# One core, two transformer-like blocks: the first norm's statistics taken token by token from x, and the first weights in two units

## The reference

```python
h = jnp.concatenate([meta, x], axis=1)            # 528 x 1024
y = xf * lax.rsqrt(jnp.mean(xf * xf, axis=-1, keepdims=True) + EPS)   # rmsnorm(h, norm1_g)
z = y * g
proj = z @ w_in[l]                                # 1024 x 5632
q, fl, iv, og, pin, ga, gb = jnp.split(proj, SPLITS, axis=-1)
```

## Time and profile before

| | us |
|---|---|
| median of three runs | 1639.83 |
| the profiled execution | 1643.81 |
| its span | 1642.0 |
| TensorE busy (matmuls) | 1563.1 (95%) |
| TensorE weight loads | 1369.9 (83%) |
| VectorE busy | 817.2 (50%) |
| ScalarE busy | 704.7 (43%) |

### The profile page before, as it was taken

The page is one execution under the profiler, slowest core; times in us unless marked ns, Lnnn a source line. Parts: engine busy times, 40 slices in busy tenths (PEclk is TensorE's granted clock), DMA queues, the critical chain, the costliest instruction groups (busy, mean ns, idle before and its releaser), DMA issues.

```text
span 1642.0 us, 24062 instructions
## 1 busy us (share of the span) xinstructions
PE 1563.1 (95%) x10314; PEld 1369.9 (83%) x10314; DVE 817.2 (50%) x1198; ACT 704.7 (43%) x1051; POOL 3.5 (0%) x14
## 2 busy tenths in 40 slices
PE   6999899999999999999999899899998999899988
PEld 5989899999998889997888667688897777678878
DVE  6376776645635445543345567532223555533243
ACT  4464666754324233232323655432222666633232
POOL 0000000000000000000000000000000000000000
PEclk9999899999998999999999999999999999799999
DMA  4421112114322323322324100122321111122222
GB/s 140 141 68 59 52 59 72 52 40 143 103 82 73 103 79 102 100 80 89 99 85 108 26 27 1 52 83 97 103 78 55 53 48 52 52 64 87 93 77 77
DMA packets 130957, 125.46 MB, mean 76 GB/s; under 512 B 20201, under 2 KB 128516, under 8 KB 130468
## 3 DMA queue, kind: packets, MB, share of 16 engines
q1 hardware_dynamic: 130388, 120.36, 23.4%
q0 software_dynamic: 464, 3.56, 0.6%
HBM read 119.66 MB, written 4.26 MB: 75 GB/s over the span
## 4 chain that ended last, share of the span: by engine, by line
PE 86%; DVE 6%; ACT 4%; issue 3%; DMA 0%; SPq 0%; DVEq 0%; ACTq 0%
PE PS L803 72%; PE PS L902 3%; PE PS L1112 2%; DVE wlo L1695 2%; PE PS L1057 2%; PE PS L1077 2%; DVE small L2169 1%; ACT Pm L1222 1%; ACT xka L1222 1%; PE PS L822 0%; PE PS L1089 0%; PE PS L914 0%; DVE PT L2193 0%; ACT L1227 0%; PE PS L1062 0%
## 5 line engine op out<-in xcount | busy, mean ns | idle before, releaser
L803 PE MATMUL PS<-zhi,whi 128*128 128x258 f32 (+2 forms) x2000 | 512.9, 318 | 20.6 <-DVE zlo L1756 10.6
L803 PE MATMUL PS<-zlo,whi 128*128 128x258 f32 (+2 forms) x2000 | 503.4, 313 | 0.0
L803 PE MATMUL PS<-zhi,wlo 128*128 128x258 f32 (+2 forms) x2000 | 502.6, 313 | 0.0
L803 PEld LDWEIGHTS PS<-zhi,whi 128*128 128x128 f32 x2000 | 330.7, 191 | 47.9 <-issue 17.5
L803 PEld LDWEIGHTS PS<-zhi,wlo 128*128 128x128 f32 x2000 | 329.7, 191 | 21.4
L803 PEld LDWEIGHTS PS<-zlo,whi 128*128 128x128 f32 x2000 | 329.8, 191 | 19.8
L1695 DVE TENSOR_TENSOR wlo<-raw,whi 128x2048 fp32r<-128x2048 f32 (+2 forms) x113 | 247.5, 2192 | 126.6 <-ACT whi L1222 126.2
L1222 ACT ACTIVATE whi<-raw 128x2048 fp32r<-128x2048 f32 (+2 forms) x113 | 207.0, 1833 | 122.4 <-DMA raw<-in_w_down 40.3
L1222 ACT ACTIVATE Pm<-PS,small 128x144 f32<-128x144 f32 (+3 forms) x128 | 68.6, 539 | 76.8 <-DVE small L2169 76.8
L2169 DVE TENSOR_REDUCE small<-PS 128x1 f32<-128x144 f32 (+3 forms) x128 | 62.5, 502 | 34.1 <-PE PS L1064 33.5
L803 PE MATMUL PS<-ghi,whi 128*128 128x512 f32 x176 | 70.4, 400 | 2.2 <-DVE glo L2064 2.2
(11 more groups left out here) (327 smaller groups left out, 2040.7 us busy)
## 6 DMA issues: line engine op xcount, KB each, us to landing
raw<-in_w_in SPq DMA_DIRECT2D x51, 1024.0 KB, 5.1
raw<-in_w_up SPq DMA_DIRECT2D x22, 1024.0 KB, 5.0
raw<-in_w_out SPq DMA_DIRECT2D x8, 1024.0 KB, 5.1
raw<-in_w_down SPq DMA_DIRECT2D x8, 1024.0 KB, 5.1
raw<-in_w_br_mla SPq DMA_DIRECT2D x4, 1024.0 KB, 5.2
raw<-in_w_br_fox SPq DMA_DIRECT2D x4, 1024.0 KB, 5.4
raw<-in_w_down SPq DMA_DIRECT2D x4, 768.0 KB, 4.5
hspill<-hT SPq DMA_DIRECT2D x1, 2112.0 KB, 12.6
```

Of the source, the lines that this page charges most:

```text
L803: ins = mm(o_, l_, r_, start=first, stop=last)
```

## The change

The sums of squares are no longer taken from the turned slices. ScalarE squares each block of 128 tokens as it lies in `xt`, tokens on partitions, and the accumulator output gives the sum of a token over all 1024 features (`xss`, 128x5: four blocks and the meta rows). Ln and Exp then work on five columns. VectorE multiplies the identity with these columns to a matrix `diag` (128x528, in each block a diagonal), and one product with ones spreads the roots over all partitions; ScalarE copies them to `rb`. x comes in four pieces of 512 KB, each with its own semaphore; slices 0 to 3 are copied to `hT` by VectorE and 4 to 7 by ScalarE. The value tiles 0 and 1 take their weights from two units of 512 rows each (`w_low(1)` stands behind slice 1 of z on VectorE), so there is one unit more. The norm's gain comes by itself, over ScalarE's queue. The other parameter rows are turned between slices 3 and 4 of the first product, and their copies, the gate bounds and the casts of the constants stand behind z. The table load is made at the start. `Norm` loses its buffers for norm 1, and the `sq` buffers go.

```diff
-    for j in range(2):
-        pair("v", A_V, j)
+    for i in range(2):
+        u = pl.unit([("w_in", i * D // 2, A_V, 256, 0)], KT // 2, 256)
+        for m in range(2):
+            pl.piece(("v", m), u, 128 * m, KT // 2, "z", slot=m, k0=i * KT // 2, first=i == 0, last=i == 1)
+    n = 2
+    pair("v", A_V, 1)
...
+        xjunk, _ = at("xjunk", [P, 5, D], F32, e - 3 * 4 * T * 4)
+        diag, _ = at("diag", [P, T], F32, e - 4 * 4 * T * 4 - 4 * 4 * (T + PADC))
...
-            for cols in (slice(0, D // 2), slice(D // 2, D)):
-                for i in range(QB):
-                    sp.dma_start(xt[:, i, cols], a["x"][0, P * i:P * (i + 1), cols])\
-                      .then_inc(x_in if cols.start == 0 else x2_in, 16)
+            for i in range(QB):
+                sp.dma_start(xt[:, i, :], a["x"][0, P * i:P * (i + 1), :]).then_inc(xt_in[i], 16)
...
-                if u == 0:
-                    for name, half, dst in ROW_LOADS:
-                        src = a[name]
-                        flat = {1: "(t p) -> t p", 2: "l (t p) -> (l t) p", 3: "l w (t p) -> (l w t) p"}[len(src.shape)]
-                        r0, n = ROWS[dst]
-                        n = 16 if name == "lb_logits" else n
-                        r0 -= P * half
-                        sp.dma_start(prow[r0:r0 + n, half, :], src.rearrange(flat, p=P)).then_inc(prm_in, 16)
                 if u == 1:
+                    for name, half, dst in ROW_LOADS[1:]:
+                        sp.dma_start(*row_load(name, half, dst)).then_inc(prm_in, 16)
+                if u == 2:
...
+            nc.gpsimd.memset(epst, EPS).then_inc(const_ready, 1)
+            nc.gpsimd.memset(xss, 1.0).then_inc(const_ready, 1)
...
-            pe.wait_ge(const_ready, 6)
-            pe.wait_ge(x_in, 16 * (QB + 1))
+            pe.wait_ge(const_ready, 5)
+            pe.wait_ge(x_in, 16)
             for k in range(KT):
-                ins = tr(PS[:, 5, NM * k:NM * (k + 1)], xm[:, P * k:P * (k + 1)], ident[0:NM, 0:NM])
+                ins = tr(PS[:, 7, NM * k:NM * (k + 1)], xm[:, P * k:P * (k + 1)], ident[0:NM, 0:NM])
             ins.then_inc(x_turned, 1)
-            for k in range(KT):
-                if k == KT // 2:
-                    pe.wait_ge(x2_in, 16 * QB)
-                if k >= 4:
-                    pe.wait_ge(h_copied, k - 4 + 2)
+            for i in range(QB):
+                if i == QB - 1:
+                    pe.wait_ge(g1_in, 16)
+                    tr(PS[:, 6, 0:KT], prow[0:KT, 0, :], ident[0:KT, 0:KT]).then_inc(prm_turned, 1)
+                pe.wait_ge(xt_in[i], 16)
+                for k in range(KT - 2):
+                    ins = tr(PS[:, k, P * i:P * (i + 1)], xt[:, i, P * k:P * (k + 1)], ident[:, :])
+                    if i == QB - 1:
+                        ins.then_inc(x_turned, 1)
+            pe.wait_ge(h_copied, 1)
+            pe.wait_ge(g1_copied, 1)
+            for k in range(KT - 2, KT):
                 for i in range(QB):
-                    ins = tr(PS[:, k % 4, P * i:P * (i + 1)], xt[:, i, P * k:P * (k + 1)], ident[:, :])
+                    ins = tr(PS[:, k, P * i:P * (i + 1)], xt[:, i, P * k:P * (k + 1)], ident[:, :])
                 ins.then_inc(x_turned, 1)
-                if k >= 3:
-                    stats_of(norm1, ones, k - 3)
-            pe.wait_ge(prm_in, PRM_DMAS)
-            tr(PS[:, 4, 0:NROW1], prow[0:NROW1, 0, :], ident[0:NROW1, 0:NROW1])
-            tr(PS[:, 4, P:P + NROW2], prow[0:NROW2, 1, :], ident[0:NROW2, 0:NROW2]).then_inc(prm_turned, 1)
-            for k in range(KT - 3, KT):
-                stats_of(norm1, ones, k)
-            pe.wait_ge(h_copied, KT + 1)
+
+            pe.wait_ge(diag_ready, 2)
+            pe.wait_ge(h_copied, 3)
+            for b in range(2):
+                ins = mm(PS[:, b, 0:HALF], ones[:, :], diag[:, HALF * b:HALF * (b + 1)], start=True, stop=True)
+            ins.then_inc(rb_spread, 1)
+            pe.wait_ge(h_copied, KT // 2 + 1)
+
+            def turn_rows():
+
+                pe.wait_ge(h_act, KT // 2)
+                pe.wait_ge(prm_in, PRM_DMAS)
+                tr(PS[:, 4, 0:NROW1], prow[0:NROW1, 0, :], ident[0:NROW1, 0:NROW1])
+                tr(PS[:, 4, P:P + NROW2], prow[0:NROW2, 1, :], ident[0:NROW2, 0:NROW2]).then_inc(prm_turned, 1)
...
                 if n == ("v", 0):
                     gemm_pair([("v", 0), ("v", 1)], norm1.z_ready)
+                    turn_rows()
+                    gemm_pair([("v", 0), ("v", 1)], norm1.z_ready, KT // 2)
+                    pe.wait_ge(prm_copied, 1)
                 elif n != ("v", 1):
                     gemm(n)
...
+            def h_out(k):
+                act.wait_ge(x_turned, k + 2)
+                A_(hT[:, k, NM:T], PS[:, k, :], ACT.Copy).then_inc(h_act, 1)
+
+            nc.scalar.dma_start(*row_load(*ROW_LOADS[0])).then_inc(g1_in, 16)
             log_exp()
+            act.wait_ge(const_ready, 2)
+            act.wait_ge(x_in, 16)
+            tick(A_(xjunk[0:NM, QB, :], xm[:, :], ACT.Square, accum_out=xss[0:NM, QB:QB + 1]))
+            for i in range(QB):
+                act.wait_ge(xt_in[i], 16)
+                tick(A_(xjunk[:, i, :], xt[:, i, :], ACT.Square, accum_out=xss[:, i:i + 1]))
+            settle()
+            tick(A_(xss, xss, ACT.Ln, scale=1.0 / D, bias=epst))
+            settle()
+            A_(xss, xss, ACT.Exp, scale=-0.5).then_inc(rs_ready, 1)
+            w_high(0)
+            h_out(4)
+            h_out(5)
+            act.wait_ge(rb_spread, 1)
+            A_(halves(rb[:, :]), PS[:, 0:2, 0:HALF], ACT.Copy).then_inc(norm1.rb_ready, 1)
+            norm_hi(norm1, 0)
+            h_out(6)
+            norm_hi(norm1, 1)
+            h_out(7)
+            w_high(1)
+            for k in range(2, KT):
+                norm_hi(norm1, k)
+            w_high(2)
             act.wait_ge(lb_sub, 1)
             A_(lbe, lbt, ACT.Exp).then_inc(lb_exp, 1)
-            w_high(0)
-            norm_rb(norm1)
-            for k in range(KT):
-                norm_hi(norm1, k)
-            w_high(1)
 
             def rec_step(p, i):
...
+            h_out(0)
+            h_out(1)
+            dve.wait_ge(rs_ready, 1)
+            dve.wait_ge(const_ready, 8)
+            V.tensor_scalar(diag[:, 0:NM], ident[:, 0:NM], xss[:, QB:QB + 1], None, ALU.mult).then_inc(diag_ready, 1)
+            V.tensor_tensor(diag[:, NM:T].rearrange("p (i c) -> p i c", i=QB),
+                            ident[:, :].unsqueeze(1).broadcast_to([P, QB, P]),
+                            xss[:, 0:QB].unsqueeze(2).broadcast_to([P, QB, P]), ALU.mult).then_inc(diag_ready, 1)
+            h_out(2)
+            h_out(3)
...
+            w_low(0)
+            dve.wait_ge(h_copied, KT // 2 + 1)
+            dve.wait_ge(g1_copied, 1)
+            for k in range(KT + 1):
+                if k < KT:
+                    if k >= 2:
+                        dve.wait_ge(norm1.z_ready, k - 1)
+                    if k >= KT // 2:
+                        dve.wait_ge(h_act, k - KT // 2 + 1)
+                    norm_zt(norm1, k)
+                if k >= 1:
+                    norm_lo(norm1, k - 1)
+                if k == 2:
+                    w_low(1)
+            for i in range(2):
+                tick(V.memset(qf[i][:, :, 0:LATE], 0.0))
+            dve.wait_ge(prm_turned, 2)
+            tick(V.tensor_copy(prm[:, KT:NROW1], PS[:, 4, KT:NROW1]))
+            V.tensor_copy(prm[:, P:P + NROW2], PS[:, 4, P:P + NROW2]).then_inc(prm_copied, 1)
             settle()
+            dve.wait_ge(prm_copied, 1)
+            w_low(2)
 
             l0, l1 = prm[:, 8:16], prm[:, 16:24]
             tick(V.tensor_tensor(lb, l0, l1, ALU.max))
...
-            w_low(0)
-            norm_split(norm1)
-            for i in range(2):
-                tick(V.memset(qf[i][:, :, 0:LATE], 0.0))
-            w_low(1)
```

More of the change, by code:

```diff
@@ L451, in build_program @@
         fsum, g12 = small[:, 96:112], small[:, 112:120]
+        xss = small[:, 120:125]
         def col(name, k):
@@ L737, in _, with gemm_pair @@
             at_piece = [0]
-            def gemm_pair(names, x_wait):
+            def gemm_pair(names, x_wait, k0=0):
                 parts = [gemm_steps(name) for name in names]
-                for k in range(KT):
-                    pe.wait_ge(x_wait, k + 1)
+                p = pl.pieces[at_piece[0] - 1]
+                for k in range(p.kt):
+                    pe.wait_ge(x_wait, k0 + k + 1)
                     ends = [step(k) for step in parts]
```

97 lines of the change are left out of this document (50 added, 47 removed).

## The result

The changed kernel takes 1628.28 us, the median of four executions (1626.6 to 1632.47). The kernel before, on the same chip, takes 1639.66 us (1639.15 to 1639.87, four executions). The ratio is 0.9935, with an interval from 0.9915 to 0.9955, so the gain lies between 7.4 and 13.9 us.

A forecast was written before the change was run, and what follows sets the result against it. TensorE, on the chain for 86% of the span, bounds the kernel; only the start can gain. Third value tile 7.95 us earlier, less 1.85 for half clock, gives 6.1: 1639.8 to 1633.7 us, range 1631.0 to 1637.2.

The forecast's parts named there:

- half clock in the third value tile: After TensorE's pause before that tile, half clock for 3.5 to 3.9 us was expected, a loss of 1.85 us.
- the way through z: Eight slices of z: extra ScalarE and VectorE work leaves 8.3 of 10.3 us gained; last low part at 29.4.
- The landing of x: Start of the kernel: the last of four pieces of x was kept at 10.95 us, as before.
- The bound of 1.2 us: Transfers of x at the start: at 365 GB/s throughout, 3 x 147 KB are saved, or 1.2 us.
- Rival 1: At the start, x lands sooner, at 365 GB/s throughout: gain 7.3 us, 1632.5 us; chance 13%.
- The chain from the landing to the first product: Head: x at 10.95, then Square, roots, diagonal, VectorE's tiles and low part; first large product at 18.2.
- the forecast's case of half clock there: Head, product with ones: result copied by 16.0 instead of 15.1 us, costing nothing because VectorE ends last.
- The seam: Between z and third value tile: third unit's split, small Exp, ScalarE's copy; tile at 34.7, 7.95 us earlier.
- rival 2: Clock stays up before the third value tile, tile finishing later or ScalarE sooner: 7.95 us, 1631.9 us; chance 9%.
- The pause around 440: Old profile: TensorE pause of some 2.3 us, then half clock 442.25 to 445.25, used to expect a clock fall.
- Costs set at nothing: Fourth unit's later load and split, spill of h, one more unit, late constants: all priced at no cost.
- the page's figure: Trainium skill's transfer rate puts x there at 7.7 us: estimate 1630.5 us, given 2 of 13 percent.

The follow-up runs named there:

- the changed kernel with one memset: The changed kernel with its first transfer held back by one VectorE memset (about 1.0 us): 1631.0 us, ratio 0.9938 to the kernel before.

## Why the prediction was right and wrong

Two steps failed, and each was a term of the sum. The last piece of x was kept at 10.95 us and landed at 8.6, which is 2.3 us. And 1.85 us were taken off for half clock in the third value tile, where the clock stayed full in every trace. A third term, the way through z, was 0.6 us too long. The rest of the chain came as forecast. The chain, step by step, from the timelines and the chain above:

| | forecast | after |
|---|---|---|
| last piece of x landed | 10.95 | 8.6 |
| its Square and sum done | 12.2 | 9.81 |
| roots done | 12.7 | 10.38 |
| diagonal done | 13.55 | 11.24 |
| VectorE free for z | 16.0 | 13.5 |
| first large product | 18.2 | 15.81 |
| last low part of z | 29.4 | 26.42 |
| third unit's low part | 32.85 | 29.91 |
| ScalarE's copy of the first tile | 33.55 | 30.42 |
| third value tile | 34.7 | 31.62 |

- **The landing of x failed.** "The new kernel asks for the same bytes in the same order of time, in four pieces, and I keep 10.95 for the last one": it was 8.6, and 2.3 us of the missing gain are here. The dip to 218 GB/s between 4 and 7 us was taken for a property of the place; it was one of the pieces' size, as the old kernel with four pieces showed. The bound of 1.2 us was worked out from 365 GB/s behind the dip and with the same number of requests ahead; 391 GB/s was reached, and the last piece was asked for 1.9 us earlier (2.60 in place of 4.50). The last part could have been read from the order of SP alone. Rival 1, that x lands sooner, came true with nearly twice its 1.2 us. The Trainium skill (DMA: Bandwidth & Descriptors, the section on a DMA's two cost components) gave an estimate of 7.7 us by its rate. The traces of the four-piece kernels have 8.6 to 9.75, so it is 0.9 to 2.1 us short; the 10.95 of the kernel before, which was held against it, was 1.2 to 2.3 us long.
- **The chain from the landing to the first product was right**, 7.25 us forecast and 7.2 measured, with VectorE as its end, as said: `rb` was there at 13.10, before VectorE had the low part done. The small product with ones ran at full clock, so the forecast's case of half clock there was not tried.
- **Through z** 11.2 us were forecast and 10.6 measured. The high and the low part of the second half unit fitted in better than thought: slice 2's low part ended 4.1 us behind the first product, where 4.7 were forecast. The five slices behind it took 6.49 us, beside 6.48.
- **The seam was right in its structure, and wrong in its clock.** Third unit, three small operations, Exp, copy: 5.3 us from the end of z to the tile forecast, 5.2 measured. But TensorE, at half clock in z, ended the pair only at 30.6, just as ScalarE came. The pause was 0.55 us in the first trace and 1.74 in the second, and behind neither did the clock fall. The 1.85 us taken off for it were not lost, which is rival 2's outcome (9%). In the first trace it came for rival 2's own reason, as the tile finished late; in the second it came against a pause almost as long as the 2.25 us that were forecast. The forecast had half clock in z "in z's own pace" and did not carry it to the moment at which TensorE is done.
- **The pause around 440 was no evidence for a fall elsewhere.** The earlier trace rows showed a fall behind some 2.3 us of standing still. The same trace held a pause of 3.36 us at 85 with no fall, which was not looked at, and other executions have them the other way round. The one trace that was read was unusual at both places: behind the 2.25 us the clock fell in 3 of 12 traces, behind the 3.36 us it stayed in 1 of 11. One profiled execution can't price a fall.
- **Costs set at nothing** held: no transfer of weights ends a wait behind z in the chain; the fourth unit, the spill and the constants don't appear there. But the margin of the fourth unit was thin, and not 8 us: it landed at 29.81 and was split from 30.91 on, and in the trace of the changed kernel with one memset ScalarE waited 0.26 us for it, beside the chain.
- **Small slips of the working.** The last eighth of x was issued at 4.50 and landed at 11.01 in the trace, not 4.45 and 10.95. Two tiles of 0.69 and a low part of 1.22 behind 13.55 make 16.15, not 16.0; the records overlap a little, and 2.25 us were measured for the three.
- **The sum** closes with this: 6.1 forecast, 2.3 from the landing, 0.6 from z, 0.1 at the seam and 1.85 from the clock make 11.0, where the medians say 10.8 and 11.4. The profiled executions differ by 17.2 us, 6.2 more than the sum. Half of the difference in busy time at half clock, 5.9 us, covers nearly all of it: draws of the clock.
- **The range** was made from the edits' bounds alone, so that two terms off the same way left it. It had no term for a spread of 7.5 us between executions either; the medians of the kernel before alone are 1639.66, 1640.87 and 1642.34 in three sets of executions. The share left for the page's figure, 2 in 100, was too small.

Left open: why sixteen transposes and one sum were slower in the old kernel with four pieces; why the last piece of x lands between 8.6 and 9.75 in executions of the same start; and what decides a draw of the clock, and why its odds differ so much from one pause to another.

## What to carry to other kernels

Price a head from the landing of its last input, and treat that landing as a quantity that the shape of the transfers changes: when an edit alters the size or the number of requests, work out the issue times anew and keep the rate of other shapes as a bound with a real chance. Before a term of the sum is taken from a fall of the clock, look at every pause of that length, in more than one trace. Expect to need many executions where a kernel has many pauses: four against four left 6.6 us between the ends of the interval here, ten against nineteen 3.1. Where TensorE waits a few microseconds for a chain of other engines, products of no use that end in time can be cheaper than the pause: filling seven pauses, together with moving the Exp, gave 6.0 us here. The same in one pause could not be told from no gain.

## What the runs showed of the hardware

- The granted clock behind one and the same pause of 3.36 us stayed at 1.00 in one execution and fell to half in another, with instructions equal around it; over the traces it fell in 10 of 11. Over nineteen executions the kernel before spread over 7.5 us, or 0.45%, and the longer executions are those with the lower mean granted clock.
- Pauses of 0.55 (twice), 1.62, 1.74 and 1.75 us at the seam were followed by no half clock. Elsewhere a pause of 1.73 us was followed by 3.4 us of half clock in 12 of 13 traces, one of 2.25 us in 3 of 12, and the two of 4.4 us in all.
- Half clock on an engine that has time to spare costs next to nothing: TensorE ran 6.8 or 3.4 us of z at 1.2 GHz, and the third value tile started 15.8 us behind the first product in both cases.
- Between 3 and 8 us, when most of x moves, the transfers ran at 267 GB/s with x in pieces of 256 KB, whose rows have 2 KB, and at 380 and 391 GB/s with x in pieces of 512 KB with rows of 4 KB.
- A float32 product of 128 by 128 by 128 took 0.22 us at full clock (6.3 us for 28), in two records.
